# Two-block transformer kernel on one core: a gate tile computed beside memory attention, weight chunks sent before modulation rows, and the opening pairs of tiles taken one by one

## The chip, the cores and the metric

One NeuronCore of a Trainium2 chip. The time is the device time of one launch in microseconds. The kernel before takes 3383.51 us (median of 3 runs, 3382.79 to 3384.63).

## The reference, cut to what matters

A first block of two layers and a second block of two layers, all in fp32, for 512 positions of width 1024.

```
# first block, each of 2 layers
h = x @ w_in[l]                          # split into the inputs of four branches, their gates, and merge
y_mem = memory attention(xq, mem)        # 4 heads, 512 queries against 256 memory tokens
proj  = einsum('bsnc,ncd->bsnd', branches, w_o_branch[l])
gates = sigmoid(merge.reshape(B, S, 4, D) + b_gate[l])
merged = sum(gates * proj, axis=2);  out = merged @ w_out[l]
x = layer_norm(alpha * x + out)
# second block, each of 2 layers: x (512 rows) and a context (256 rows)
mod = silu(c) @ w_ada[i] + b_ada[i]      # for x and, with c_ctx, for the context
hx = rms_norm(x) * (1 + sc1) + sh1;  zx = hx @ w_in[i]     # q, k, v, pool and fourier inputs
hc = the same of the context;        zc = hc @ w_in[i]     # layer 1: its k and v only
x = x + ga1 * (mix(zx) @ w_out[i])
x = x + ga2 * swiglu(rms_norm(x) * (1 + sc2) + sh2)        # layer 0: the context too
```

## The kernel before, in words

**Three matmuls for one.** Activations lie transposed, 128 channels to a tile, 512 positions (256 for the context) along the free axis. Each fp32 operand is split into a rounded `high` and the rest, `low`, and a product is high x high + high x low + low x high, summed in a PSUM bank. A tile of 128 output channels over 1024 inputs is 8 k-steps of 3, 24 matmuls. `with_high` (L153) issues the two that need the weights' high alone, `three` (L161) all three in a row.

**The stream of weights** (L93). All weights lie in memory as one sequence of chunks of 128x1024, in the order of use. SP loads them into a ring of 3 (`send`, L105), and waits with chunk n for the low of chunk n-3. ACT makes a chunk's high (`hi`, L115, L123), POOL its low (`lo`, L126, L131). Highs and lows have two buffers each, so the high of a chunk waits until the next-but-one before it is done with: TensorE counts `used` up with the first matmul of each chunk, and the split of the s-th chunk waits until the chunk after the (s-2)-th has started. Each engine works through its own instructions in the order in which they are written, and every stage is a block that starts when all engines are done with the last one.

**Memory attention** (`attention`, L275, called at L1590): 8 pairs of heads and query blocks. TensorE makes the scores two pairs ahead (L330), DVE the maximum (L447), ACT the exponent (L384), DVE the inverse of the sum (L453), POOL multiplies by it (L428), TensorE turns the probabilities round (L343), ACT and DVE copy them out (L393, L463), TensorE forms the product (L357) and DVE evicts and gates it (L468). Scores use PSUM banks 0 to 3, turns 4 and 5, products 6 and 7 in turn. POOL first gates the convolution branch (L1583). Another attention of the kernel passes `beside`, tiles of 24 matmuls put between its steps in three pieces, and then uses bank 6 alone for products.

**Merge** (L1618): for each of 8 output tiles m, four gates (24 matmuls each, `gemm3`, L670, over x) and two chunks of branch projections, n = 0, 1 and n = 2, 3 (L1653 to L1661), in the order gate, gate, projections, gate, gate, projections; chunks lie in that order (`chunks1`, L2816). ACT first splits the branches (L1672), which DVE completes (L1707), then applies the sigmoids (L1683) with the splits of later chunks between (L1684); at i = 0 it also splits branches 8 to 15 and applies `Silu` to the two condition vectors (L1692). DVE multiplies and adds (L1718, L1723), and between these works through 48 modulation rows (512 KB each, L1731). SP sends the rows (L1634) into four buffers, a row when DVE has used up the one four before, and a weight chunk ahead of most rows (L1629).

**Second block, input stage** (L2200 on). ACT makes the norm's scale, then for each of 8 tiles DVE normalises (L2125), ACT shifts and rounds to the high (L2105), DVE makes the low (L2133); all of x's tiles come before the context's. In layer 0 only x is done so, the context was done earlier. `first_pair` (L2138) runs the first two output tiles of x as these arrive; then come tiles 2 to 10 (L2272), each waiting for its chunk's low, with the context's products beside x's (layer 1: from tile 4 on). ACT evicts each tile (L2354) and makes a chunk's high after that (L2376). `used` for the pair's second chunk is counted with its last matmul.

**Feed-forward** (L2680 on): the same norm (`norm.scalar`, L2107) and `first_pair`, for x and the context in layer 0 and for x in layer 1, then pairs of gate and up tiles (L2711); ACT applies `Silu` (L2729).

## Time and profile before

| | |
|---|---|
| median of 3 runs | 3383.51 us |
| profiled execution | 3376.45 us |
| its span, first to last instruction | 3374.7 us |
| mean granted TensorE clock | 0.989 |
| TensorE busy | 3210.8 us (95%) |
| VectorE (DVE) | 1502.5 us (45%) |
| ScalarE (ACT) | 1185.3 us (35%) |
| GpSimd (POOL) | 1494.4 us (44%) |

Times are microseconds from the start of the span. PE is TensorE, L12 is line 12 of the kernel. A timeline row has the start, the length, the engine, the line and the operation, output <- inputs, how many instructions were merged, and in brackets how long the engine had been idle before it and what ended that. Matmuls overlap: each is shown with its whole length, so eight 128x512 matmuls that start 0.23 us apart are shown with 0.39 us each. A granted clock of 1.00 is TensorE's 2.4 GHz, 0.50 is 1.2 GHz.

### The profile page before, as it was taken

How to read it: one execution, taken by the hardware profiler on the slowest of the kernel's cores; microseconds unless marked ns; L12 is line 12 of the kernel's file. 1: busy time of each engine (PE TensorE's matmuls, PEld its weight loads, DVE VectorE, ACT ScalarE, POOL GpSimd, SP SyncE). 2: the span in 40 equal slices, each digit the busy share in tenths (PEclk: the TensorE clock that was granted, in tenths of full speed). 3: DMA queues.
4: the chain of work that ended last, by engine and by line, in shares of the span. 5: the costliest groups of instructions: out<-in, count | busy, mean ns of one | idle time of the engine just before them, and what ended most of it. 6: DMA issues, size and time to landing. Idle time of an engine off the chain costs nothing. (4 is left out here: it accounts for less than half of the span.)

```text
span 3374.7 us, 51787 instructions
## 1 busy us (share of the span) xinstructions
PE 3210.8 (95%) x21120; PEld 2520.3 (75%) x21120; DVE 1502.5 (45%) x2374; ACT 1185.3 (35%) x1940; POOL 1494.4 (44%) x820
## 2 busy tenths in 40 slices
PE   8899999999999999989998989999999988899999
PEld 6784786788668747868886756888888865678787
DVE  7643374899575332948986235300100022620000
ACT  6224434422352434252225445322122233532221
POOL 4432553455353235535543276344234424745454
PEclk9999999999999999999999999999999999999999
DMA  3011132555210111335543200121122211023232
GB/s 129 8 34 56 57 100 68 207 200 194 80 63 4 46 56 57 106 109 191 206 150 109 72 26 26 51 68 60 54 74 65 63 54 50 7 88 96 92 99 94
DMA packets 77611, 284.18 MB, mean 84 GB/s; under 512 B 8736, under 2 KB 8736, under 8 KB 76864
## 3 DMA queue, kind: packets, MB, share of 16 engines
q1 hardware_dynamic: 77376, 280.88, 24.9%
q8 instruction: 168, 2.75, 0.3%
q14 instruction: 67, 0.55, 0.1%
HBM read 278.75 MB, written 2.10 MB: 83 GB/s over the span
## 5 line engine op out<-in xcount | busy, mean ns | idle before, releaser
L131 POOL TENSOR_TENSOR lows<-ring,highs 128x1024 fp32r<-128x1024 f32 x376 | 946.3, 2518 | 1555.5 <-ACT highs L123 1519.5
L155 PE MATMUL ps<-x_high,highs 128*128 128x512 f32 x1936 | 772.4, 399 | 32.7 <-ACT highs L123 14.1
L158 PE MATMUL ps<-x_low,highs 128*128 128x512 f32 x1936 | 759.9, 393 | 0.0
L123 ACT ACTIVATE highs<-ring 128x1024 fp32r<-128x1024 f32 x376 | 396.9, 1056 | 742.4 <-PE ps L155 382.1
L155 PEld LDWEIGHTS ps<-x_high,highs 128*128 128x128 f32 x1936 | 366.4, 189 | 124.3 <-issue 29.3
L158 PEld LDWEIGHTS ps<-x_low,highs 128*128 128x128 f32 x1936 | 366.4, 189 | 78.2 <-issue 2.9
L1731 DVE CUSTOM_DVE_ANT_0 BR<-BR 128x1024 f32<-128x1024 f32 x144 | 282.6, 1963 | 6.8
L2762 DVE TENSOR_TENSOR hidden_scratch<-ps,hidden_scratch 128x512 f32<-128x512 f32 x44 | 30.4, 691 | 545.9 <-PE ps L2081 541.9
L677 PE MATMUL ps<-x_high,lows 128*128 128x512 f32 x1040 | 256.9, 389 | 0.0
L677 PEld LDWEIGHTS ps<-x_high,lows 128*128 128x128 f32 x1040 | 195.2, 188 | 40.6
L2638 DVE SCALAR_TENSOR_TENSOR BR<-ps,mod,BR 128x512 f32<-128x512 f32 x72 | 47.4, 661 | 368.8 <-PE ps L167 368.8
L167 PE MATMUL ps<-hidden_parts,lows 128*128 128x512 f32 (+1 forms) x528 | 188.9, 358 | 0.0
L163 PE MATMUL ps<-hidden_parts,highs 128*128 128x512 f32 (+1 forms) x528 | 188.8, 358 | 0.0
L166 PE MATMUL ps<-hidden_parts,highs 128*128 128x512 f32 (+1 forms) x528 | 188.8, 358 | 0.0
L428 POOL TENSOR_SCALAR tiles<-tiles 128x768 f32<-128x768 f32 (+1 forms) x80 | 155.0, 1950 | 27.9 <-DVE tiles L453 27.9
L2081 PE MATMUL ps<-x_high,lows 128*128 128x512 f32 x672 | 167.1, 391 | 0.0
L1558 DVE SCALAR_TENSOR_TENSOR ps<-X,par,ps 128x512 f32<-128x512 f32 x232 | 152.9, 751 | 0.0
L2081 PEld LDWEIGHTS ps<-x_high,lows 128*128 128x128 f32 x672 | 123.3, 188 | 24.0
L428 POOL TENSOR_SCALAR X<-X 128x256 f32<-128x256 f32 (+3 forms) x96 | 97.8, 1033 | 66.2 <-DVE X L453 66.2
L447 DVE TENSOR_REDUCE tiles<-ps 128x1 f32<-128x768 f32 (+1 forms) x80 | 67.6, 846 | 108.7 <-PE ps L330 108.5
L1683 ACT ACTIVATE BR<-ps,par 128x512 f32<-128x512 f32 x64 | 44.1, 689 | 201.2 <-PE ps L677 201.1
L166 PEld LDWEIGHTS ps<-hidden_parts,highs 128*128 128x128 f32 x528 | 99.4, 188 | 16.1
(437 smaller groups left out, 5847.0 us busy)
## 6 DMA issues: line engine op xcount, KB each, us to landing
ring<-in_w SPq DMA_DIRECT2D x414, 512.0 KB, 3.5
BR<-in_ada SPq DMA_DIRECT2D x72, 512.0 KB, 3.5
merging<-in_ada SPq DMA_DIRECT2D x24, 512.0 KB, 3.5
X<-in_xT SPq DMA_DIRECT2D x4, 512.0 KB, 6.8
X<-in_memT SPq DMA_DIRECT2D x2, 1024.0 KB, 5.5
BR<-in_cond SPq DMA_DIRECT2D x4, 512.0 KB, 5.4
out<-BR SPq DMA_DIRECT2D x8, 256.0 KB, 4.4
cst<-in_cst SPq DMA_DIRECT2D x1, 1408.0 KB, 7.9
```

The lines of the kernel that those rows point to most:

```text
L123: nc.scalar.activation(self.high(n), self.chunk(n), ACT.Copy).then_inc(self.hi_made, 1)
L131: nc.gpsimd.tensor_tensor(self.low(n), self.chunk(n), self.high(n).bitcast(F32), ALU.subtract).then_inc(self.lo_made, 1)
L155: mm = nc.tensor.matmul(ps, high, xhigh, start=start, stop=False)
L158: nc.tensor.matmul(ps, high, xlow, start=False, stop=False)
L163: mm = nc.tensor.matmul(ps, high, xhigh, start=start, stop=False)
L166: nc.tensor.matmul(ps, high, xlow, start=False, stop=False)
L167: return nc.tensor.matmul(ps, low, xhigh, start=False, stop=stop)
L428: nc.gpsimd.tensor_scalar(prob(i, u), prob(i, u), stats[:, 3, n:n + 1], None, ALU.mult).then_inc(S("normed"), 1)
L677: mm = nc.tensor.matmul(PS[:, bank, :], tile_of(stream.low(n), k), xh[:, k, :], start=False, stop=(k == DK - 1))
L1558: ins = v.scalar_tensor_tensor(out=ACC[:, c, :] if tap == TAPS - 1 else acc, in0=H0[:, c, tap:tap + T], scalar=w, in1=acc, op0=ALU.mult, o ...
L1731: v.tensor_tensor_reduce(PROD, rows_of(t), CB[:, c, :], 1.0, 0.0, ALU.mult, ALU.add, AD[:, t, c:c + 1]).then_inc(S("ada"), 1)
L2081: mm = nc.tensor.matmul(ps, tile_of(stream.low(n), k), high[:, k, :], start=False, stop=(k == DK - 1))
```

## The change

1. `attention` takes `ahead`. For memory attention that is the first gate tile of the merge (m = 0, branch 0), in three pieces of 8 matmuls into PSUM bank 7: two ahead of the scores of pair 2 and of pair 3, the third (its lows) ahead of the turns of pair 7. SP sends two more chunks in that stage, ACT makes one high (i = 0) and POOL one low (between pairs 6 and 7). Products then use bank 6 alone.
2. In the merge the first gate is left out and its sigmoid reads bank 7. The chunks of m = 0 lie in the order gate, gate, gate, projections, gate, projections. SP sends each weight chunk one step earlier relative to the modulation rows. `Silu` on the condition comes after the sigmoid of i = 2.
3. `first_pair`: for the last stream the two tiles run one after the other, from k = 4 on for x alone and from k = 0 for the context, and `used` is counted when the second one starts alone.
4. `norm.scalar` makes the third chunk's high right after the shifted tiles of a stream (`between`), and in layer 1's input stage evicts x's first two tiles there, before the context's shifted tiles.
5. Tiles 2 to 10 of the input stage run their 16 (with the context 32) matmuls with the weights' high first and wait for the low after them.

```diff
+class Ahead:
+        self.at = {(0, 0): 0, (0, 1): 1, (8, 1): 2}
+    def send(self, sp):
+        self.stream.send(sp, self.first + RING + 1)
+    def tensor(self, pe, i, slot):
...
+        if part < 2:
+            stream.wait_high(pe, n)
+            for k in range(4 * part, 4 * part + 4):
+                with_high(self.nc, bank, tile_of(stream.high(n), k), self.high[:, k, :], self.low[:, k, :], k == 0, stream.used if k == 0 else None)
+        else:
+            stream.wait_split(pe, n)
+            for k in range(DK):
+                self.nc.tensor.matmul(bank, tile_of(stream.low(n), k), self.high[:, k, :], start=False, stop=(k == DK - 1))
+    def scalar(self, act, i):
+        if i == 0:
+            self.stream.hi(self.nc, act, self.first + 2)
+    def pool(self, pool, i):
+        if i == 6:
+            self.stream.lo(self.nc, pool, self.first + 2)
...
-        return 6 if beside is not None else 6 + g % 2
+        return 6 if beside is not None or ahead is not None else 6 + g % 2
...
-                if beside is not None and p.group >= 1:
+                if (beside is not None or ahead is not None) and p.group >= 1:
                     pe.wait_ge(S("out"), p.group)
...
         def gate_chunk(i):
-            return n0 + 6 * (i // 4) + 3 * (i % 4 // 2) + i % 2
+            return n0 + (0, 1, 2, 4)[i] if i < 4 else n0 + 6 * (i // 4) + 3 * (i % 4 // 2) + i % 2
+        def branch_chunk(m, n):
+            return n0 + 6 * m + 3 * (n // 2) + 2 if m else n0 + 3 + n
+        def splits_ahead(i):
+            return (n0 + 4, n0 + 5, n0 + 6, n0 + 8)[i] if i < 4 else min(gate_chunk(i) + (4 if i % 2 else 3), n0 + 48 + 1)
...
-                    stream.send(sp, n0 + RING + max(45 * t // 48, min(t, 2)))
+                    stream.send(sp, n0 + RING + max(45 * t // 48 + 1, min(t + 2, 4)))
...
-                        for i in (4 * m + n, 4 * m + n + 1):
+                        for i in ((4 * m + n, 4 * m + n + 1) if m else (1, 2) if n == 0 else (3,)):
...
-                stream.hi(nc, act, gate_chunk(1) + 1)
+                stream.hi(nc, act, n0 + 3)
...
-                    act.wait_ge(S("gate_product"), i + 1)
+                    if i:
+                        act.wait_ge(S("gate_product"), i)
...
-                    stream.hi(nc, act, min(gate_chunk(i) + (4 if i % 2 else 3), n0 + 48 + 1))
+                    stream.hi(nc, act, splits_ahead(i))
...
                     if i == 0:
                         for b in range(8, 16):
                             branch_high(b)
+                    if i == 2:
                         act.wait_ge(S("cond"), 32)
                         nc.scalar.activation(CB, CB, ACT.Silu).then_inc(S("silu_c"), 1)
...
-                for s in self.sts:
+                for i, s in enumerate(self.sts):
                     self.shifted(act, s)
+                    if i == between:
+                        stream.hi(nc, act, upto + 1)
+                        for take in then:
+                            take()
...
                 for i, s in enumerate(sts):
-                    for k in range(DK):
+                    final = i == len(sts) - 1
+                    half = DK if not final else 4 if i == 0 else 0
+                    for k, j in [(k, j) for k in range(half) for j in range(2)] + [(k, j) for j in range(2) for k in range(half, DK)]:
...
-                            if j == 1 and i == len(sts) - 1 and k == DK - 1:
+                        if j == 1 and final and k == half:
                                 mark = used
...
-                    stream.wait_split(pe, n)
-                    first = True
+                    stream.wait_high(pe, n)
+                    taking = []
...
-                            mm = three(nc, PS[:, s["bank"] + i % 2, 0:s["n"]], tile_of(stream.high(n), k), tile_of(stream.low(n), k),
-                                       s["h"][:, k, :], s["l"][:, k, :], k == 0, k == DK - 1, mark(n, first))
+                            with_high(nc, bank, tile_of(stream.high(n), k), s["h"][:, k, :], s["l"][:, k, :], k == 0, mark(n, k == 0 and not taking))
+                        taking.append((s, bank))
+                    stream.wait_split(pe, n)
+                    for s, bank in taking:
+                        for k in range(DK):
+                            mm = nc.tensor.matmul(bank, tile_of(stream.low(n), k), s["h"][:, k, :], start=False, stop=(k == DK - 1))
+                        mm.then_inc(S("product" + s["name"]), 1)
...
-                norm.scalar(act, n0 + PARTS)
+                norm.scalar(act, n0 + PARTS, 0, () if layer == 0 else (lambda: evict(streams[0], tiles[0]), lambda: evict(streams[0], tiles[1])))
...
-                        norm.scalar(act, n0 + PARTS)
+                        norm.scalar(act, n0 + PARTS, len(full) - 1)
```

## Rows read from the trace of the kernel before

**Rows 1.** The page: its first line and TensorE's part of section 1.
```profile
span 3374.7 us, 51787 instructions
...
PE 3210.8 (95%) x21120; PEld 2520.3 (75%) x21120; DVE 1502.5 (45%) x2374; ACT 1185.3 (35%) x1940; POOL 1494.4 (44%) x820
```
**Rows 2.** TensorE's waits: us in total, times, longest.
```profile
PE ps L155 <- ACT highs L123: 17.5, 9, 7.4
```
**Rows 3.** Timeline of TensorE, memory attention of layer 0.
```profile
560.66 1.97 PE L330 MATMUL ps<-X 128*128 128x256 f32 x8 [1.26 <-PEq L1459]
563.59 2.17 PE L330 MATMUL ps<-X 128*128 128x256 f32 x8 [0.96 <-ACT X L384]
...
567.45 0.44 PE L343 MATMUL ps<-cst,X 128*128 128x128 f32 x2 [0.46 <-POOL X L428]
...
581.09 0.44 PE L343 MATMUL ps<-cst,X 128*128 128x128 f32 x2 [1.33 <-POOL X L428]
...
585.25 1.13 PE L357 MATMUL ps<-X 128*128 128x128 f32 x8 [0.63 <-issue]
```
**Rows 4.** Timeline of TensorE, start of the merge of layer 0.
```profile
587.42 0.61 PE L155 MATMUL ps<-x_high,highs 128*128 128x512 f32 x1 [1.05 <-PEq L314]
...
592.76 1.98 PE L677 MATMUL ps<-x_high,lows 128*128 128x512 f32 x8
594.58 0.39 PE L155 MATMUL ps<-x_high,highs 128*128 128x512 f32 x1
...
607.34 0.50 PE L155 MATMUL ps<-x_high,highs 128*128 128x512 f32 x1 [1.54 <-ACT highs L123]
```
**Rows 5.** Timeline, input stage of the second block's layer 0, DVE and TensorE.
```profile
1858.20 1.62 DVE L2133 SCALAR_TENSOR_TENSOR x_low<-tiles,mod,x_high 128x512 fp32r<-128x512 f32 x2
...
1865.64 0.50 PE L163 MATMUL ps<-x_high,highs 128*128 128x512 f32 x1 [3.37 <-POOL lows L131]
```
**Rows 6.** Timeline, input stage of the second block's layer 1, ACT and TensorE.
```profile
2746.57 0.91 ACT L2105 ACTIVATE context_high<-tiles,mod 128x256 fp32r<-128x256 f32 x2 [1.22 <-DVE tiles L2125]
...
2752.40 0.58 ACT L2354 ACTIVATE tiles<-ps 128x512 f32<-128x512 f32 x1
...
2756.39 0.79 PE L163 MATMUL ps<-x_high,highs 128*128 128x512 f32 x1 [6.18 <-POOL lows L131]
...
2769.96 0.39 PE L163 MATMUL ps<-x_high,highs 128*128 128x512 f32 x1
```
**Rows 7.** Timeline, feed-forward openings of layers 0 and 1, TensorE and DVE.
```profile
2163.65 3.83 PE L2142 MATMUL ps<-highs 128*128 128x512 f32 x10 [1.88 <-PEq L2650]
...
2184.18 0.49 DVE L2133 SCALAR_TENSOR_TENSOR context_low<-BR,mod,context_high 128x256 fp32r<-128x256 f32 x1 [0.19 <-ACT context_high L2105]
...
2187.33 0.50 PE L155 MATMUL ps<-x_high,highs 128*128 128x512 f32 x1 [1.31 <-ACT highs L123]
...
3017.58 0.50 PE L155 MATMUL ps<-x_high,highs 128*128 128x512 f32 x1 [0.95 <-ACT highs L123]
```
**Rows 8.** Timeline of ACT, merge of layer 0.
```profile
606.24 1.05 ACT L123 ACTIVATE highs<-ring 128x1024 fp32r<-128x1024 f32 x1
```
**Rows 9.** Timeline of POOL, end of attention and start of the merge, layer 0.
```profile
580.11 3.63 POOL L428 TENSOR_SCALAR X<-X 128x256 f32<-128x256 f32 x4 [1.65 <-DVE X L453]
588.60 2.39 POOL L131 TENSOR_TENSOR lows<-ring,highs 128x1024 fp32r<-128x1024 f32 x1 [4.86 <-ACT highs L123]
```
**Rows 10.** Busy time by stretch: us, each engine busy (instructions), clock, DMA, GB/s.
```profile
587.40:590.80 3.40, 3.38 (x8) 2.64 (x9) 1.73 (x1) 3.34 (x6) 2.21 (x1) 0.53 0.49 148
...
1532.00:1770.00 238.00, 237.90 (x1036) 194.16 (x1035) 217.37 (x241) 66.37 (x79) 117.23 (x42) 1.00 0.51 181
```
**Rows 11.** Timeline of SP and TensorE, tenth tile of the merge of layer 0.
```profile
629.61 0.43 SPq L112 DMA_DIRECT2D ring<-in_w  x1
...
644.17 1.98 PE L677 MATMUL ps<-x_high,lows 128*128 128x512 f32 x8
```
**Rows 12.** DMA issues from 587 to 625 us: count, KB each, median us to landing.
```profile
ring<-in_w SPq DMA_DIRECT2D x7, 512.0 KB, 4.5
```

More of the change, by code:

```diff
@@ L272, in pool, with __init__, attention @@
         self.stream.lo(self.nc, pool, self.first + min(piece // 3, len(self.places) - 1) + 2)
-def attention(nc, stage, PS, ident, causal, pairs, results, scale, probs, probsT, small, gates=None, opening=None, beside=None):
+class Ahead:
+    def __init__(self, nc, stream, bank, first, high, low):
+        self.nc, self.stream, self.bank, self.first, self.high, self.low = nc, stream, bank, first, high, low
+        self.at = {(0, 0): 0, (0, 1): 1, (8, 1): 2}
+    def send(self, sp):
+        self.stream.send(sp, self.first + RING + 1)
+    def tensor(self, pe, i, slot):
+        if (i, slot) not in self.at:
+            return
+        stream, n, bank, part = self.stream, self.first, self.bank, self.at[i, slot]
+        if part < 2:
[12 more added lines that the diff above has]
+            self.stream.lo(self.nc, pool, self.first + 2)
+def attention(nc, stage, PS, ident, causal, pairs, results, scale, probs, probsT, small, gates=None, opening=None, beside=None, ahead=None):
     S, other = stage()
@@ L318, in _ @@
                 beside.send(sp)
+            if ahead is not None:
+                ahead.send(sp)
             clear(sp, other)
@@ L362, in _ @@
             for i in range(N + 2):
+                if ahead is not None:
+                    ahead.tensor(pe, i, 0)
                 if i + lead < N:
@@ L366, in _ @@
                     beside.tensor(pe, S, 2 * i)
+                if ahead is not None:
+                    ahead.tensor(pe, i, 1)
                 if 1 <= i <= N:
@@ L370, in _ @@
                     beside.tensor(pe, S, 2 * i + 1)
+                if ahead is not None:
+                    ahead.tensor(pe, i, 2)
                 if i >= 2:
@@ L405, in _ @@
                     exponent(i + 1)
+                if ahead is not None:
+                    ahead.scalar(act, i)
                 if beside is not None:
@@ L430, in _ @@
                     beside.pool(pool, 2 * i + 1)
+                if ahead is not None:
+                    ahead.pool(pool, i)
         @block.vector
@@ L1592, in first @@
                   128.0 ** -0.5, [XT(0), XT(1), XT(2)], [XT(4), XT(5)], XT(14),
-                  [GLATER[:, 4 + 2 * (g // 2):6 + 2 * (g // 2), 256 * (g % 2):256 * (g % 2) + 256] for g in range(4)], gate_conv)
+                  [GLATER[:, 4 + 2 * (g // 2):6 + 2 * (g // 2), 256 * (g % 2):256 * (g % 2) + 256] for g in range(4)], gate_conv,
+                  ahead=Ahead(nc, stream, PS[:, 7, :], base + FIRST["merge"], XH, XL))
         room.close()
@@ L2145, in first_pair @@
                 for i, s in enumerate(sts):
[L2146 removed]
+                    final = i == len(sts) - 1
+                    half = DK if not final else 4 if i == 0 else 0
+                    for k, j in [(k, j) for k in range(half) for j in range(2)] + [(k, j) for j in range(2) for k in range(half, DK)]:
                         self.ready(pe, s, k)
[L2148 to L2155 removed]
+                        mark = opened if j == 0 and i == 0 and k == 0 else None
+                        if j == 1 and final and k == half:
+                            mark = used
+                        mm = three(nc, PS[:, s["bank"] + banks[j], 0:s["n"]], tile_of(stream.high(n + j), k), tile_of(stream.low(n + j), k),
+                                   s["h"][:, k, :], s["l"][:, k, :], k == 0, k == DK - 1, mark)
+                        if k == DK - 1:
+                            mm.then_inc(done(j, s), 1)
             def ready(self, pe, s, k):
@@ L2373, in _ @@
                     for s in streams:
-                        if t in plan[s["name"]] and not (layer == 0 and s["name"] == "c" and j < EARLY):
+                        if t in plan[s["name"]] and not (layer == 0 and s["name"] == "c" and j < EARLY) and not (layer and j < 2):
                             evict(s, t)
```

21 lines of the change are left out of this document (8 added, 13 removed).

## The prediction

> **What bounds the kernel now.** I read the page first: TensorE is busy for 3210.8 of 3374.7 us [rows 1]. So only what fills a TensorE gap, or keeps its clock up, can pay; the matmuls themselves stay the same in number. Second, TensorE's waits, by who ended them: ACT's `highs` cost the streamed gemms 17.5 us in 9 waits [rows 2]: late splits of weight chunks. Third, the timeline at the places that the diff touches. In memory attention TensorE waits in small pieces: 0.96, 0.46, 1.33 and 0.63 us among them [rows 3], about 5.4 us in all over 26 us. In the merge stage it waits 1.54 us once [rows 4]. In the second block's input stage it waits 3.37 us in layer 0 [rows 5] and 6.18 us in layer 1 [rows 6]; at the two opening pairs of the feed-forward 1.31 and 0.95 us [rows 7]. The last number to take along is the pitch of a 128x512 matmul at full clock: eight from 592.76 to 594.58 make 0.2275 us each [rows 4]; a tile of 24 is 5.46 us.
>
> **Part 1, the gate tile beside attention, in both layers of the first block.**
> Removed from the merge: 24 matmuls, 5.46 us. Removed too: the wait of 1.54 us. There a high was made at 606.24 only, behind `Silu` and two table loads [rows 4, 8]. The change moves `Silu` behind two more sigmoids and two more highs, and sends chunk n0+3 in the stage before. By my estimate (from the stage's start, with the durations of ACT's rows), ACT then makes the highs of n0+3, n0+4, n0+5 at 9.5, 15.5 and 17.2 us, where TensorE wants them at 10.9, 16.5 and 21.9; `Silu` ends at 20.4, and n0+6 is ready at 25 for 27.5. So the wait should not come back; the least room is 1 us, at n0+4, where the weights queue behind the two condition vectors.
> Added to attention: the same 24 matmuls in three pieces of 8 (1.82 us each), one split on ACT (1.05) and one on POOL. The first two pieces stand ahead of the scores of pairs 2 and 3. TensorE was free at 562.6; two pieces and two pairs of scores (2.0 us) end at 568.2, the first two transposes at 568.6, where the next stood at 567.45 [rows 3]. Delay: 1.15 us, and from there TensorE had no rest for 7 us, so it is passed on. The third piece and POOL's split come at the end. POOL is the one that is waited for there: its normalisations of pairs 6 and 7 run back to back in 3.63 us, and the transpose at 581.09 waits for them [rows 3, 9]. The split is put between the two and takes 2.39 us [rows 9], so pair 7, its transposes and its product come 2.3 us later; the third piece fits into that wait at no cost of its own. Stage longer by 1.15 + 2.3 = 3.4 us; bounds 0 (all in the gaps) and 5.46 (nothing hidden). I take 3.4. The single output bank (6 alone, since 7 holds the gate) makes the products of a new group wait for the eviction before; those waits of about half a microsecond fall where TensorE waits for POOL anyway.
> Sum: 5.46 + 1.54 - 3.4 = 3.6 us a layer, **7.2 us** for two.
> After the gap at the stage's start the granted clock was 0.53 for 3.4 us, the 1.2 GHz level; TensorE had stood still for 0.63 and 1.05 us before and done little between [rows 3, 4, 10]. Eight matmuls at 0.427 instead of 0.2275 cost 1.6 us. I leave that in place, as the gap stays; if it goes, 3.2 us more for two layers.
>
> **Part 2, the opening pairs.** `first_pair` used to alternate its two tiles over k; now the last stream's second tile (all of it for the context, k 4 to 7 for a lone x) runs when the first is done. Its mark allows the split of the third chunk, and comes some 11 matmuls before the end instead of at the end. `norm.scalar` makes that split before anything else, and the input stage no longer waits for `lows` before a tile's first 16 matmuls. The price: TensorE must wait for the last k of the first tile, then still has 12 matmuls (24 for the context) to do.
> Layer 0, input: the last x_low ends at 1859.82 [rows 5]. After 0.05 us (a high that ended at 607.29 let TensorE start at 607.34 [rows 4, 8]) come 3 and 12 matmuls, 3.4 us: the pair ends at 1863.3, 1.2 us later than before, and the third tile starts there, its high made since 1862.1. Before it started at 1865.64. Gain **2.4 us**.
> Layer 1, input: TensorE lagged here, so the pair ends as before, at 2750.2 less what the pipeline overlaps (2756.39 - 6.18) [rows 6]. The third tile follows at once and ends at 2755.5. But ACT now evicts x's second tile (done 2750.25, 0.5 us) **before** the context's eight shifted tiles, which took from 2746.57 to 2752.40, 5.83 us [rows 6]. They end at 2756.6, then comes the fourth chunk's high, 1.05: the fourth tile starts at 2757.65, after a new wait of 2.1 us, and the fifth at 2763.1, where it was 2769.96 [rows 6]. Gain **6.8 us**. Part of it is clock: that third tile took 8.1 us for 24 matmuls before (2769.96 - 5.46 - 2756.39), 2.7 more than at full clock.
> Feed-forward, layer 0: the context's last low ends at 2184.67; 3 + 24 matmuls of half width (half of 0.2275) make 3.1, so the third tile starts at 2187.8 against 2187.33 [rows 7]: **loss 0.5 us**, though its wait of 1.31 is gone. Layer 1: the pair is 1.2 us longer as in layer 0's input, the wait of 0.95 goes: **0**, between -0.3 and +0.2.
> Moving lows behind highs also makes both streams' products of a tile end close together; evictions come later by up to 1.9 us. TensorE needs them a tile later, with two banks a stream: nothing.
> The clock again. A gap of 1.88 us was followed by ten matmuls in 3.83 us, 0.38 each, mostly the lower level [rows 7]; after the one of 3.37 us the next began no slower [rows 5]. So the new wait of 2.1 us may or may not cost a stretch of 1.7 us; I take half of it, 0.9.
> The Trainium skill (TensorE: Matmul & The Clock Gate, HAM oscillation) blames long unbroken gaps alone for the lower level; by that rule the new wait costs nothing and the sum would be 0.9 larger. The rows disagree with a rule by length alone: the longer gap cost less than the shorter.
>
> **Sum:** 7.2 + 2.4 + 6.8 - 0.5 - 0 - 0.9 = **15.0 us**. The profiled execution took 3376.45 us (span 3374.7), 7.1 below the median of the timed runs, 3383.51; the terms are differences within it, so I take them off both: 3361.5 for a profiled one, **3368.5 us** for the median.
>
> **Rivals.**
> (A) The gate tile is not hidden: attention grows by the whole 5.46, as TensorE's pieces hold up scores on which DVE, ACT and POOL all wait. For it: the gaps are all shorter than a piece of 1.82 us. Against: POOL's chain at the end leaves 1.33 and the split's 2.3. Gain 15.0 - 4.1 = 10.9: 3372.6. With the clock also lost at the feed-forward's context pair (1.7, as TensorE rests there half of 4 us) and the whole stretch at the new wait: 3375.
> (B) The clock holds at both merges and at the new wait: 15.0 + 3.2 + 0.9: 3364.4.
> (C) TensorE outruns its weights in the merge. They are sent between modulation rows, which go out as DVE uses them up. In the tenth tile of the stage the chunk sent at 629.61 landed 4.5 us later, was wanted at 640.5 (644.17 less 16 matmuls) and needs 1.05 for its high: room 5.4 us [rows 11, 12]. TensorE gains 7.0 on this, `Silu` starts 3.5 later, one send ahead gives back a row's time, about 5: room -0.1 if DVE makes up nothing; but it idled for 20.6 of 238 us [rows 10], so 2 or 3 us are left. If it bites, it gives back up to 3 a layer: 3374.5.
> (D) Slower: the rows starve. SP now waits for a later chunk's low before each row, and all 44 paced rows of a layer queue behind that wait. Each wait that is not covered delays DVE's modulation sums. DVE has 20.6 us to spare in the merge [rows 10], and 7.5 a layer must be lost to undo the gains; so it decides from (20.6 + 7.5)/44 = 0.64 us a row. At 1 us a row the kernel loses 23.4 - 7.5 a layer, 32 in all: 3415. Against it: 4 row buffers, and by my count the low in question is made two tiles before DVE wants the row.
> (E) The change does not do what it says: the splits were hidden anyway and only the order differs. Excluded in the input stages by their waits; for the feed-forward pairs I already count it so.
>
> **Numbers.** Forecast 0.58, A 0.16, B 0.12, C 0.09, D 0.05. About 0.2% (6.8 us) is what a measurement of this kernel can tell from no change. A and C together can fall into it: same 0.08; D gives slower 0.05; faster 0.87. The range takes in B with a shorter attention (2 x 1.5 more) at 3361 and A with C at 3377; the bounds 0 and 5.46 of the attention term lie inside.
>
> **What would show it.** Attention 3.4 us longer in each layer, its two split matmul pieces ahead of scores. No wait of 1.54 in the merge, none for a high in its first six tiles. In layer 0's input stage the third tile right behind the pair; in layer 1 no wait of 6.18 but one of some 2.1 before the fourth tile, ended by ACT's highs. In the feed-forward's opening, TensorE waiting in pieces for context_low and the third tile no earlier. I am wrong if attention is as long as before or 5 us longer, if DVE waits for rows, or if SP's queue makes ACT wait for the ring.

## The result, and the profile after

| | kernel before | changed kernel |
|---|---|---|
| first measurement, median | 3384.07 us (3382.79 to 3388.82, 4 runs) | 3361.91 us (3359.74 to 3364.15, 4 runs) |
| second measurement, median | 3384.05 us (3376.86 to 3394.47, 24 runs) | 3365.16 us (3362.82 to 3368.75, 6 runs) |
| profiled execution, span | 3376.45, 3374.7 us | 3363.31, 3361.5 us |

The ratio is 0.9932, 95% interval 0.9915 to 0.9949, in the first measurement and 0.9943, 0.9928 to 0.9957, in the second: 22 and 19 us less. The profiled pair differs by 13.2 us of span only. How the three figures go together is told under "What the runs showed of the hardware".

First the page of the changed kernel, as in [rows 1], and TensorE's wait for ACT's `highs`, as in [rows 2]:

```profile
span 3361.5 us, 51793 instructions
...
PE 3210.8 (96%) x21120; PEld 2519.1 (75%) x21120; DVE 1510.7 (45%) x2374; ACT 1184.6 (35%) x1940; POOL 1490.9 (44%) x820
```
```profile
PE ps L155 <- ACT highs L123: 17.5, 9, 7.4
```

TensorE's busy time is the same 3210.8 us to the tenth: no work was saved, gaps were. And the wait that the change was aimed at stands at 17.5 us in 9 waits as before. A sum of waits is a poor witness here. Four of the nine are gone (1.54 twice, 1.31, 0.95 us) and four new ones have come (1.13, 1.09, 0.54, 2.01 us, shown below); the waits for POOL's `lows`, 9.5 us before, are what left the list.

So I read it by stage instead. The length of a stage here is the time from TensorE's first instruction in it to its first in the next, from the timelines:

| stage | before | after | measured | forecast |
|---|---|---|---|---|
| memory attention, layer 0 / 1 | 26.76 / 26.76 | 29.56 / 29.57 | +2.80 / +2.81 | +3.4 each |
| merge, layer 0 / 1 | 276.32 / 276.32 | 267.47 / 270.93 | -8.85 / -5.39 | -7.0 each |
| input stage, layer 0 | 131.05 | 128.87 | -2.18 | -2.4 |
| input stage, layer 1 | 98.35 | 93.12 | -5.23 | -6.8 + 0.9 |
| feed-forward to its last up tile, layer 0 / 1 | 285.42 / 189.23 | 286.00 / 189.28 | +0.58 / +0.05 | +0.5 / 0 |
| sum | | | **-15.4** | -15.0 |

The other stages, which the change doesn't touch, became 2.2 us longer in this pair; they have 63 us at the lower clock where the kernel before has 48.

The timeline of TensorE in the changed kernel's memory attention, layer 0, against [rows 3]:

```profile
560.56 1.97 PE L365 MATMUL ps<-X 128*128 128x256 f32 x8 [1.27 <-PEq L1504]
562.18 0.58 PE L155 MATMUL ps<-x_high,highs 128*128 128x512 f32 x1
...
568.23 1.03 PE L365 MATMUL ps<-X 128*128 128x256 f32 x4
...
579.56 1.13 PE L392 MATMUL ps<-X 128*128 128x128 f32 x8 [0.78 <-DVE BR L513]
...
581.60 0.44 PE L378 MATMUL ps<-cst,X 128*128 128x128 f32 x2 [0.69 <-POOL X L471]
...
582.90 2.09 PE L297 MATMUL ps<-x_high,lows 128*128 128x512 f32 x8
585.76 0.44 PE L378 MATMUL ps<-cst,X 128*128 128x128 f32 x2 [0.78 <-POOL X L471]
...
587.94 1.13 PE L392 MATMUL ps<-X 128*128 128x128 f32 x8 [0.63 <-issue]
590.12 0.47 PE L155 MATMUL ps<-x_high,highs 128*128 128x512 f32 x1 [1.05 <-PEq L347]
```

The gate tile's pieces start at 562.18 without a gap; L378 are the turns, L392 the products, L297 the third piece, with a wait for POOL's normalisation before it (0.69 us, at 581.60) and after it (0.78 us). At 579.56 the single output bank shows: a wait of 0.78 us for DVE's eviction. The last row is the start of the merge. POOL in the same stretch, against [rows 9]:

```profile
580.62 1.83 POOL L471 TENSOR_SCALAR X<-X 128x256 f32<-128x256 f32 x2 [1.43 <-DVE X L498]
582.41 2.40 POOL L131 TENSOR_TENSOR lows<-ring,highs 128x1024 fp32r<-128x1024 f32 x1
584.79 1.82 POOL L471 TENSOR_SCALAR X<-X 128x256 f32<-128x256 f32 x2
```

The low parts the normalisations of pairs 6 and 7, and the turns at 585.76 follow the second of them. Now TensorE at the openings of the two input stages, against [rows 5, 6]:

```profile
1854.29 0.50 PE L163 MATMUL ps<-x_high,highs 128*128 128x512 f32 x1 [0.36 <-DVE x_low L2193]
...
1858.70 0.39 PE L155 MATMUL ps<-x_high,highs 128*128 128x512 f32 x1
...
2747.31 1.98 PE L2366 MATMUL ps<-x_high,lows 128*128 128x512 f32 x8
2751.29 0.74 PE L155 MATMUL ps<-x_high,highs 128*128 128x512 f32 x1 [2.01 <-ACT highs L123]
2751.82 0.63 PE L158 MATMUL ps<-x_low,highs 128*128 128x512 f32 x1
```

In layer 0 the third tile (1858.70) follows the pair with no wait; the 3.37 us are gone. In layer 1 the 6.18 us are gone, and a new wait of 2.01 us stands before the fourth tile, with matmuls of 0.63 us behind it: the lower clock.

### The profile page after: what moved, and what is told of

Read it like the earlier page. It is cut to its first block and busy times, and to the rows that moved or that the text cites. A ratio compares the mean times of both kernels' runs of the same rounds, so it can differ in the third digit from the quotient of the medians.

```text
span 3361.5 us, 51793 instructions
## 1 busy us (share of the span) xinstructions
PE 3210.8 (96%) x21120; PEld 2519.1 (75%) x21120; DVE 1510.7 (45%) x2374; ACT 1184.6 (35%) x1940; POOL 1490.9 (44%) x820
## 3 DMA queue, kind: packets, MB, share of 16 engines
q1 hardware_dynamic: 77376, 280.88, 24.4%
## 5 line engine op out<-in xcount | busy, mean ns | idle before, releaser
L155 PE MATMUL ps<-x_high,highs 128*128 128x512 f32 x2080 | 832.4, 400 | 32.1 <-ACT highs L123 13.5
L158 PE MATMUL ps<-x_low,highs 128*128 128x512 f32 x2080 | 815.9, 392 | 0.0
L155 PEld LDWEIGHTS ps<-x_high,highs 128*128 128x128 f32 x2080 | 393.3, 189 | 130.7 <-issue 35.2
L158 PEld LDWEIGHTS ps<-x_low,highs 128*128 128x128 f32 x2080 | 393.4, 189 | 85.5 <-issue 4.8
L1787 DVE CUSTOM_DVE_ANT_0 BR<-BR 128x1024 f32<-128x1024 f32 x144 | 290.4, 2017 | 6.8
L166 PEld LDWEIGHTS ps<-hidden_parts,highs 128*128 128x128 f32 x528 | 99.4, 188 | 16.1
L163 PEld LDWEIGHTS ps<-hidden_parts,highs 128*128 128x128 f32 x528 | 99.4, 188 | 16.1
```

What stands on the lines that cost most here:

```text
L155: mm = nc.tensor.matmul(ps, high, xhigh, start=start, stop=False)
L158: nc.tensor.matmul(ps, high, xlow, start=False, stop=False)
L163: mm = nc.tensor.matmul(ps, high, xhigh, start=start, stop=False)
L166: nc.tensor.matmul(ps, high, xlow, start=False, stop=False)
L1787: v.tensor_tensor_reduce(PROD, rows_of(t), CB[:, c, :], 1.0, 0.0, ALU.mult, ALU.add, AD[:, t, c:c + 1]).then_inc(S("ada"), 1)
```

## The experiments

All kernels are compared with the kernel before on the same chip. Experiments 5 to 10 are one execution each. Against the kernel before on their chip they took, in this order, 17.1, 22.1, 19.3, 17.2, 18.5 and 16.2 us less (3381.20 us once for 5, 6, 7 and 9, a median of 3384.75 for 8 and 10); the changed kernel itself ran from 3359.7 to 3368.8 us, so these totals don't tell the edits apart. Each is read by the length of the stages that its edit touches, against the first profile of the changed kernel.

**1 and 2. Each half alone.** `gate_only` has the gate tile, the order of chunks, the sends and the place of `Silu`; `opening_only` has the rest (`first_pair`, `norm.scalar`, the tiles of the input stage).

```diff
# gate_only keeps, of the changed kernel:
+                  ahead=Ahead(nc, stream, PS[:, 7, :], base + FIRST["merge"], XH, XL))
# opening_only keeps:
+                    half = DK if not final else 4 if i == 0 else 0
```

> The kernel before with the gate tile beside memory attention and the changed sends and order of the merge, and with the opening pairs and the input stages as they were. My theory: attention 2.8 us longer and the merge 8.8 (layer 0) and 5.5 us (layer 1) shorter, as in the profile of the changed kernel, so 8.5 to 9 us less than before; 5 to 6 of it if the clock falls at the merges' starts again. Rival (the gate tile's 24 matmuls are not hidden and the gain is in the opening pairs): 3 us less.

> The kernel before with the changed opening pairs, splits and evictions of the second block alone. My theory: input stages 2.2 us (layer 0) and 5.2 us (layer 1) shorter, the feed-forward opening of layer 0 0.5 us longer, that of layer 1 even: 6 to 8 us less than before. Rival (the new order of the pairs costs as much as the earlier split brings): 0 to 3 us less.

Measured: `gate_only` 3373.21 us, ratio 0.9972 (0.9954 to 0.9990), 10.8 us less; attention 29.56, merge 267.44 and 270.93 us, the same as in the changed kernel. The rival of 3 us is out by these lengths. The median gained somewhat more than the 8.5 to 9 us expected, but its interval runs from 3 to 16 us. TensorE's waits in it still have the input stages':

```profile
PE ps L163 <- POOL lows L131: 9.5, 2, 6.2
```

`opening_only` 3375.82 us, ratio 0.9969 (0.9958 to 0.9980), 8.2 us less; input stages 128.88 and 93.55, feed-forward 286.01 and 189.28. The rival (0 to 3 us) is outside the interval, 6.8 to 14.2 us. The two parts add up: 10.8 + 8.2 = 19.0, beside the 18.9 of the whole. So close an agreement is luck with intervals as wide as these; what shows that the parts share no cover is that the stages that each half touches have, within 0.5 us, the length that they have in the changed kernel.

**3 and 4. Both kernels again**, unchanged.

> The kernel before, unchanged, profiled a second time. The first profiled execution took 3376.45 us, the timed ones 3382.8 to 3388.8. Theory 1 (that one profiled execution happened to have fewer stretches at the lower clock level than most): the ratio to the kernel before is 1.000 within 0.002, and single executions scatter over some 8 us, with the granted clock of the stretches after gaps differing from one to the next. Theory 2 (the timed executions differ from the profiled ones in something else): the profile is again near 3376 while the times stay near 3384.

> The changed kernel, unchanged. Its first profiled execution took 3363.3 us, 13.1 less than the profiled one of before, while the medians lie 22 us apart. Theory 1 (the change is worth the 13 to 15 us that the terms give, and the rest is how the chip happened to grant the clock to the executions compared): 12 to 17 us less than before here. Theory 2 (the change gains 22 us, for instance by clock stretches that only some executions of before have): 20 us or more less.

Measured: the kernel before 3385.29 us, ratio to itself 1.0004 (0.9992 to 1.0015); the changed one as in the table above, 18.9 us less. The first pair of theories is decided: the ratio is 1.000, and the profiled execution took 3391.88 us, not 3376 again; single executions scatter over 15 to 18 us, though, not over 8. The second pair isn't: 18.9 us lies between the 12 to 17 of one and the 20 of the other, and its interval, 14.6 to 24.4 us, holds both. The value is in the second profile of the kernel before, span 3390.1 us where the first had 3374.7. TensorE in its merge of layer 0, against the wait of 1.54 us in [rows 4]:

```profile
609.31 0.50 PE L155 MATMUL ps<-x_high,highs 128*128 128x512 f32 x1 [3.17 <-ACT highs L123]
609.64 0.52 PE L158 MATMUL ps<-x_low,highs 128*128 128x512 f32 x1
609.96 0.63 PE L155 MATMUL ps<-x_high,highs 128*128 128x512 f32 x1
```

This merge began at full clock (it was granted up to 609.8), and the wait is 1.6 us longer for it: the high comes when ACT comes to it, however early TensorE is. So in the kernel before a lower clock at the merge's start costs nothing, since the wait swallows it; and after the longer wait the lower clock came anyway (0.63 us a matmul), which makes this merge 277.92 us where the first profile has 276.32.

**5. The pair's second tile alone later** (`pair_split_later`).

```diff
-                    half = DK if not final else 4 if i == 0 else 0
+                    half = DK if not final else 6 if i == 0 else 4
```

> The changed kernel with the opening pairs split later: x alone from k = 6 instead of 4, the context from k = 4 instead of 0. My theory (the changed pair ends late because the second tile's matmuls come after the last low, and the third tile only needs its high about 2.2 us after that low): the layer 0 feed-forward stage 1.2 us shorter than in the changed kernel (286.0 from its first matmul to that of the second half), the layer 0 input stage 1.0 us shorter (128.9), the layer 1 feed-forward 1.0 us (189.3), the layer 1 input stage the same within 0.3 apart from the clock. Rival (the early mark is what counts, and a later split brings the wait for highs back): each 0 to 1 us longer.

Measured: 3364.12 us. Feed-forward 285.60 and 188.79: 0.4 and 0.5 us less. Input stage of layer 0 130.45, of which a stretch of lower clock ahead of the pair is 1.8; of layer 1 91.48, with no lower clock behind its wait. A new wait appears there, before the third tile:

```profile
2745.45 0.47 PE L155 MATMUL ps<-x_high,highs 128*128 128x512 f32 x1 [0.65 <-ACT tiles L2419]
```

The third tile goes to the bank of the first, and now comes before ACT has evicted that (L2419). Layer 0's input stage has the same wait (0.91 us), and gains 0.2 us instead of 1.0: in the input stages the end of the pair is worth less than I thought, since the eviction is next in line. In the feed-forward the gain here is a third to a half of the expected 1.2 and 1.0, but experiment 11 has the same edit of the pair and there these stages are 1.2 and 0.9 us shorter. No wait for the eviction stands in either. The stretches at the lower clock lie differently in the two executions (in layer 0 from 5.6 us into the stage here, from 0.9 us there; in layer 1 6.8 us long here, 3.4 there); that this is the reason was not tested.

**6. The fourth chunk's high amid the context's tiles** (`context_after_high`), in `norm.scalar` for the second stream.

```diff
                 for i, s in enumerate(self.sts):
+                    if i and then:
+                        self.shifted(act, s, 0, 4)
+                        stream.hi(nc, act, upto + 2)
+                        self.shifted(act, s, 4)
+                        continue
                     self.shifted(act, s)
```

> The changed kernel with the fourth chunk's high made between the fourth and the fifth of the context's shifted tiles, in layer 1's input stage. My theory (the wait of 2.01 us before the fourth tile is ACT's order: two evictions and eight shifted tiles stand before that high): that wait goes, and the stretch at the lower clock after it, so the stage (93.1 us from its first matmul to the next stage's) is 2.0 us shorter, 3.6 if the clock stays. Rival (the weights' arrival or DVE sets that high): no difference, and if the context's last tiles come late, a wait at the fifth tile.

Measured: 3359.07 us; the stage 89.44 us, 3.7 less than in the changed kernel. ACT, then TensorE:

```profile
2746.02 0.51 ACT L2161 ACTIVATE context_high<-tiles,mod 128x256 fp32r<-128x256 f32 x1 [0.28 <-DVE tiles L2190]
2746.43 1.05 ACT L123 ACTIVATE highs<-ring 128x1024 fp32r<-128x1024 f32 x1
2747.38 0.89 ACT L2161 ACTIVATE context_high<-tiles,mod 128x256 fp32r<-128x256 f32 x2
```
```profile
2746.71 1.98 PE L2371 MATMUL ps<-x_high,lows 128*128 128x512 f32 x8
2748.52 0.39 PE L155 MATMUL ps<-x_high,highs 128*128 128x512 f32 x1
```

Against the third tile's last eight matmuls the high starts 0.3 us before (2746.43 to 2746.71) instead of 2.9 us behind (2750.20 to 2747.31). The fourth tile follows the third without a wait, and the 2.0 us of wait and the 1.7 us of lower clock behind it are both gone. ACT's tiles of 0.51 us came 0.79 apart, waiting for DVE each time, so the high fitted into time that ACT didn't use.

**7. POOL's low one pair earlier** (`low_before_pair6`).

```diff
-        if i == 6:
+        if i == 5:
             self.stream.lo(self.nc, pool, self.first + 2)
```

> The changed kernel with POOL's split of the second gate chunk put before the normalisations of pair 6 instead of those of pair 7. My theory (memory attention is 2.8 us longer because that split of 2.4 us stands between two normalisations that are waited for, while POOL idles 1.65 us before pair 6): attention 28.3 us instead of 29.56 in each layer, 2.5 us in all. Rival (the first two matmul pieces before the scores make the stage longer): no difference.

Measured: 3361.92 us; attention 29.44 and 29.45, 0.12 us less a layer. The forecast failed. POOL did as it should; TensorE shows why it doesn't pay:

```profile
580.32 2.35 POOL L131 TENSOR_TENSOR lows<-ring,highs 128x1024 fp32r<-128x1024 f32 x1
582.65 3.63 POOL L471 TENSOR_SCALAR X<-X 128x256 f32<-128x256 f32 x4
```
```profile
583.63 0.44 PE L378 MATMUL ps<-cst,X 128*128 128x128 f32 x2 [1.55 <-POOL X L471]
...
584.94 2.09 PE L297 MATMUL ps<-x_high,lows 128*128 128x512 f32 x8
586.87 0.38 PE L378 MATMUL ps<-cst,X 128*128 128x128 f32 x2
```

The wait for the low moved with it, from pair 7's turns to pair 6's (1.55 us), while the third piece stayed ahead of pair 7's turns, where nothing is waited for any more: it stands unhidden. Here low and piece cover each other only in the same gap.

**8. Both moved** (`low_and_piece`): the edit above, and

```diff
-        self.at = {(0, 0): 0, (0, 1): 1, (8, 1): 2}
+        self.at = {(0, 0): 0, (0, 1): 1, (7, 1): 2}
```

> The changed kernel, but in memory attention POOL makes the gate chunk's low between pairs 5 and 6 instead of 6 and 7, and TensorE takes the tile's third piece ahead of pair 6's turns instead of pair 7's. My theory after low_before_pair6: there POOL ended 1.5 us earlier, but the third piece then stood unhidden ahead of pair 7's turns, and pair 6's turns waited 1.55 us for POOL; the low and the piece have to move together. Expected: attention 28.0 us in each layer (29.56 in the changed kernel, 26.76 before), all else as in the changed kernel. Rival: the low costs POOL's chain its 2.4 us wherever it stands ahead of the last pair, and the piece covers nothing new: attention stays at 29.4 to 29.6.

Measured: 3367.55 us; attention 28.94 and 28.93, 0.6 us less a layer, between the theory's 28.0 and the rival's 29.4. TensorE at the end:

```profile
585.07 0.44 PE L378 MATMUL ps<-cst,X 128*128 128x128 f32 x2 [0.22 <-POOL X L471]
586.12 1.13 PE L392 MATMUL ps<-X 128*128 128x128 f32 x8 [0.62 <-ACT X L434]
...
588.11 1.13 PE L392 MATMUL ps<-X 128*128 128x128 f32 x8 [0.63 <-issue]
```

The wait for POOL has shrunk to 0.22 us, and next in line are ACT's copies of the turned blocks (L434), 0.62 us. So moving low and piece is worth 0.6 us here. Attention is still 2.2 us longer than in the kernel before; how that divides between the pieces, the low and the copies was not separated.

**9. The next high ahead of the wait for the merged tile** (`high_before_merged`). In the changed kernel's merge of layer 1 TensorE waits three times for a high, which it didn't before. One of these places, ACT, then TensorE:

```profile
1570.80 0.63 ACT L1742 ACTIVATE merged_high<-BR 128x512 fp32r<-128x512 f32 x1 [8.21 <-DVE BR L1779]
1571.34 0.67 ACT L1738 ACTIVATE BR<-ps,par 128x512 f32<-128x512 f32 x1
1571.91 1.04 ACT L123 ACTIVATE highs<-ring 128x1024 fp32r<-128x1024 f32 x1
```
```profile
1573.10 0.47 PE L155 MATMUL ps<-x_high,highs 128*128 128x512 f32 x1 [1.13 <-ACT highs L123]
```

ACT stood still for 8.21 us, waiting for DVE to finish the merged tile, with the sigmoid and the high queued behind that wait. The other two places look the same: ACT waits 7.22 and 7.62 us for the merged tile, then TensorE 1.09 and 0.54 us for the high. In the kernel before ACT waits there too, 34.7 us in 12 with 4.9 at most, and TensorE doesn't.

```diff
                     if i >= 4 and i % 4 == 0:
+                        stream.hi(nc, act, splits_ahead(i) + 1)
                         act.wait_ge(S("merged"), 3 * i // 4)
```

> The changed kernel, where at each output tile of the merge ACT makes one chunk's high more before it waits for DVE's merged tile. My theory (the waits of 1.13, 1.09 and 0.54 us in layer 1's merge come from ACT standing in the wait for the merged tile, up to 8.2 us, as DVE is behind with its modulation sums): these waits go, that stage 2.8 us shorter than 270.9, layer 0's merge unchanged at 267.4 (269.1 with the lower clock at its start). Rival (the ring is late, since SP sends weights between rows as DVE uses them up): the same waits remain, put down to the ring.

Measured: 3362.70 us; merge of layer 1 267.44 us, 3.5 us shorter where I expected 2.8, with none of the three waits. ACT's wait for DVE's merged tile, in the changed kernel and then in this one:

```profile
ACT merged_high L1742 <- DVE BR L1779: 81.6, 14, 8.2
```
```profile
ACT merged_high L1743 <- DVE BR L1780: 9.7, 9, 2.6
```

The gain doesn't show in the single time, since layer 0's merge (269.10) had the lower clock at its start and layer 1's input stage 10.2 us of it in its opening (94.22). The three waits stood in layer 1 in all seven profiles that have the gate tile and the changed sends without this edit, and in layer 0 in one of them (`low_and_piece`: 271.08); with it, in none of four merges (two in this kernel, two in `all_four`).

**10. Sends at the old pace** (`sends_as_before`).

```diff
-                    stream.send(sp, n0 + RING + max(45 * t // 48 + 1, min(t + 2, 4)))
+                    stream.send(sp, n0 + RING + max(45 * t // 48, min(t + 2, 4)))
```

> The changed kernel, but from the fifth modulation row on SP sends the weight chunks at the pace of the kernel before (45 t / 48), one later than the changed kernel does; the first rows keep the changed order. This asks what the third part of the title, weights sent ahead of the rows, buys. My theory, after high_before_merged: the stalls of layer 1's merge come from DVE's lag through ACT's order, not from late loads, so the send order buys nothing outside the first tiles: merge stages 267.4 and 270.9 us, as in the changed kernel, with its three short waits in layer 1, each within 0.5 us. Rival (the prediction's C): the room was used up by the shorter stage, so without the earlier send TensorE waits for ACT's highs and ACT for the ring's loads, in the middle tiles: merge stages 2 us or more longer in each layer, and ACT's waits for DMA grow from near nothing to over 3 us a layer.

Measured: 3368.59 us; merges 271.13 and 270.03. My theory was wrong here and the rival right in kind for a late weight chunk: ACT now waits for one, and TensorE for ACT. But in layer 1 the stage is 0.9 us shorter than in the changed kernel, which neither foresaw.

```profile
627.86 1.06 ACT L123 ACTIVATE highs<-ring 128x1024 fp32r<-128x1024 f32 x1 [9.56 <-DMA ring<-in_w]
```
```profile
629.06 0.47 PE L155 MATMUL ps<-x_high,highs 128*128 128x512 f32 x1 [1.77 <-ACT highs L123]
```

It happens once a layer, 35 to 37 us into the stage (1.77 and 1.79 us), not all along it. Inside the two merges ACT's waits for the ring are 43.1 us in 10, where the changed kernel has 12.4 in 4 and the kernel before 4.3 in 1. The three waits of experiment 9 are absent here, but for one of 0.30 us in layer 1. So the earlier sends take away a wait of 1.8 us a layer, but in layer 1 the three waits that stand in their kernel cost more (2.76 us): they pay in layer 0 and, as long as experiment 9's edit is missing, not in layer 1. Of layer 0's 3.7 us, 1.6 are the lower clock at the stage's start. Sends at the old pace together with experiment 9's edit were not run.

**11. All four together** (`all_four`): experiments 5, 6, 8 and 9 in one kernel.

> The changed kernel with all that the single runs bore out: the low between pairs 5 and 6 with the third piece ahead of pair 6's turns; in the merge the next high ahead of the wait for DVE's merged tile; in layer 1's input stage the fourth chunk's high amid the context's shifted tiles; and the opening pairs' second tile starting alone later (k 6 for a lone x, k 4 for the context). Expected from the single runs, each against the changed kernel's 3363.3 us profiled: attention -1.5 in each of two layers, merge of layer 1 -3.5, layer 1's input stage -3.7, opening pairs -1.1 in three stages together (-0.2, -0.4, -0.5): 11.3 us less, so a ratio to the kernel before of 0.9943 - 0.0033 = 0.991, some 3354 us beside 3384. The rival is that the parts share one cover: they sit in different stages, so they should add up, except in layer 1's input stage, where the pair and the high meet: there the gain could be 2 us smaller, 0.9916.

Measured: 3353.72 us (3352.49 to 3356.78, 4 runs) against 3384.75, ratio 0.9911 (0.9894 to 0.9927): 31 us less than before, and some 8 to 11 us less than the changed kernel by its two medians, which were taken on other occasions. Attention 28.97 and 28.96, merge 267.47 and 267.46, input stages 130.74 and 90.46, feed-forward 284.79 and 188.37. The time is the 3354 us that I expected, but the terms are not: attention gave 0.6 us a layer where I had 1.5, the input stage of layer 1 2.7 instead of 3.7 (the third tile's wait of 0.65 us from experiment 5 and a further stretch of lower clock in the opening), the feed-forward 2.1 instead of 0.9; the input stage of layer 0 is 1.9 longer, with 3.4 us at the lower clock and a wait of 0.91 us for the eviction; only the merge of layer 1 gave its 3.5. The touched stages are 7.6 us shorter in all, not 11.3, so that the total agrees is partly luck. TensorE's waits for ACT's highs, 17.5 us in 9 in the kernel before and in the changed one, now:

```profile
PE ps L155 <- ACT highs L123: 12.4, 5, 7.5
```

## Why the prediction was right, and where it was off

The forecast was 3368.5 us and the range 3361 to 3377; the medians are 3361.9 and 3365.2. The direction and the places and mechanisms of the gains hold; new waits in layer 1's merge were missed. Both medians lie nearer to rival B's 3364.4 than to the forecast. B's condition, full clock at both merges, was met in the first profile and not in the second, and at the new wait in neither. Stage by stage the sum is 15.4 us against 15.0; but layer 0's merge gained 1.9 us more and layer 1's 1.6 us less than forecast, and attention cost 1.2 less in both layers together where the second input stage gained 0.7 less; so the sum agrees better than its terms, and that part is luck.

- **Attention, two pieces ahead of scores.** I took 1.15 us of delay. The scores behind the turns of [rows 3], at 567.72 before (the first row below), start at 568.23: 0.5 us. The first piece begins at 562.18, while the last scores are still running (I had it begin when they end, 562.6), and four turns run back to back in 0.44 us, where I let the first two take 0.4. Error 0.6 us a layer.
- **Attention, the low between pairs 6 and 7.** 2.3 us forecast; 2.80 - 0.5 leaves 2.3. The rows say the same: from pair 6's turns to pair 7's it was 1.80 us before (581.09 of [rows 3] to the second row below) and is 4.16 now (581.60 to 585.76), 2.36 more. That the third piece costs nothing of its own holds for this place, not for the one tried in experiment 7.

```profile
567.72 1.03 PE L330 MATMUL ps<-X 128*128 128x256 f32 x4
...
582.89 0.44 PE L343 MATMUL ps<-cst,X 128*128 128x128 f32 x2 [0.25 <-POOL X L428]
```

- **Merge.** 5.46 + 1.54 = 7.0 us was right for equal clocks: `after_again`, whose merge starts at the lower clock as the kernel before's did, has 269.07, 7.25 less. In the first profile the stretch was absent and the merge 8.85 shorter; rival B had 7.0 + 1.6 = 8.6. The step that failed is "I leave that in place": whether it comes is a matter of the execution. And rival B had the right reason for counting it: only with the wait gone does the clock there change the time.
- **Merge of layer 1, new waits.** 2.76 us, forecast as "none". I had followed ACT's order for the first tiles only. The step missing was what stands ahead of the high from i = 4 on, at every fourth i: the wait for DVE's merged tile. DVE is busy for 253.60 us of the 265 from 1495 to 1760, so it has little to catch up with. Experiment 9 shows the step. Why layer 1 has these waits and layer 0 mostly hasn't stays open (see the last section).
- **Rival C**, weights that come late, did not reach TensorE. One of my signs of being wrong did show: ACT waits for the ring inside the merges, 12.4 us in four waits, the longest 5.7, where it waited 4.3 us once before; but no wait of TensorE follows these. With the old pace of sends one does (experiment 10), at 1.8 us a layer where I priced up to 3. **Rival D**, rows that starve, did not happen: in the trace DVE never waits for a row in the merges. **Rival A** is out: attention grew by 2.8, not 5.46. For A with C together I wrote 3377 as the range's end; my own prices, 4.1 and 6 us off the gain, give 3378.6.
- **Input stage of layer 0.** 2.4 forecast, 2.18 measured. Where the old 3.37 us were followed by the lower clock the gain is larger: 4.8 against the second profile of the kernel before (133.67 us), 3.8 against `gate_only` (132.63).
- **Input stage of layer 1.** 5.9 net forecast; 5.23 here, 5.51 and 5.27 between the other pairs of profiles (98.82 to 93.31; 98.82 to 93.55). The new wait is 2.01 us where I had 2.1, and the clock stretch behind it came in whole, 1.7, where I took half. That accounts for the difference.
- **Feed-forward.** +0.5 and 0 forecast, +0.58 and +0.05 measured.
- **From the profiled pair to the median.** I took the differences of one profiled execution off the median. The interval of the second measurement holds 15.4 us (it runs from 14.6 to 24.4 us), that of the first doesn't (17.3 to 28.8). The second pair of profiles, `before_again` and `after_again`, differs by 28.5 us: 19.6 in the stages of the table and 8.9 in stages that nothing changed. So a good part of what one comparison shows beyond the sum has nothing to do with the change; that the clock accounts for all of it is not shown.

## What to carry to other kernels

When a wait in a saturated stream is removed, look at what the same engine's queue has further on: here the high's maker (ACT) had a wait for a slower engine ahead of it, which cost TensorE nothing in the kernel before, and moving one split ahead of that wait gave the 3.5 us back. Work put beside other work is best put in the very gap that its own input opens: here low and third piece moved together gained, the low alone hardly. And judge differences under half a per cent by the length of stages and by medians of many runs, never by one pair of profiles or by the sum of a wait.

## What the runs showed of the hardware that I had not expected

**The clock differs between executions of one program.** The kernel before ran from 3376.9 to 3394.5 us in 24 runs. Its two profiles, spans 3374.7 and 3390.1, have TensorE at its lower level, 1.2 GHz, for 72 and 106 us in all; the two of the changed kernel have 76 and 69. The same gap goes either way: at the merge's start TensorE stood still for 1.05 us in every profile, and the matmuls after it were at full clock in the one of `gate_only` and fell to the lower one in `after_again`; the 3.37 us of [rows 5] were followed by full clock in the first profile of the kernel before and by the lower one in the second and in `gate_only`. The Trainium skill (TensorE: Matmul & The Clock Gate, HAM oscillation) blames long unbroken gaps; the gap of 2.0 to 2.3 us before the fourth tile was followed by the lower clock in seven of the eight profiles that have it and by full clock in `pair_split_later`, and that of 3.37 us once was not followed by the lower one, so length alone doesn't settle it here.

**A removed wait can pay twice where a stretch at the lower clock follows it**: 3.7 us in experiment 6, for a wait of 2.0. That is one execution; in `all_four` the same wait is gone, but a stretch at the lower clock stands at another place of that stage.

**One pair of profiles misjudges such a difference.** The mean granted clock is 0.986 and 0.988 in the two middle runs of the kernel before's 24, and 0.989 to 0.991 in the six of the changed one. The first profile of the kernel before, at 0.989, was among its best executions, and in it the stages that nothing changed were 7.8 us shorter than in the second. That goes the right way for 13 us by the first pair of profiles and 19 to 22 by the medians; an exact account it is not.

**DVE and POOL make each other wait, and the one that starts first is not slowed.** DVE's modulation sum over 128x1024 and POOL's low of the same size in the merge of layer 1, changed kernel:

```profile
1562.23 1.22 DVE L1787 CUSTOM_DVE_ANT_0 BR<-BR 128x1024 f32<-128x1024 f32 x1
...
1563.49 3.29 DVE L1787 CUSTOM_DVE_ANT_0 BR<-BR 128x1024 f32<-128x1024 f32 x1
...
1566.93 1.23 DVE L1787 CUSTOM_DVE_ANT_0 BR<-BR 128x1024 f32<-128x1024 f32 x1
```
```profile
1562.68 3.03 POOL L131 TENSOR_TENSOR lows<-ring,highs 128x1024 fp32r<-128x1024 f32 x1 [2.79 <-ACT highs L123]
```

The first sum runs beside the low from 1562.68 to 1563.45 and still takes 1.22 us. The middle one starts when the low is already running, and takes 3.29: it ends 1.1 us after the low, which ends at 1565.71. The low in turn began while the first sum ran, and takes 3.03 us instead of the 2.40 that it took in attention. This holds for all 192 sums of the two merges of the changed kernel. The 80 that began while an instruction of POOL was running took 2.08 to 3.40 us and ended 1.08 to 1.09 us behind it; the 65 during which one of POOL began, and the 47 beside none, all took 1.21 to 1.23. So DVE's load in the merge depends on how lows and sums fall together: its sums (L1787, with the short reads of their results) are busy for 191.06 us in layer 0's merge and 194.80 in layer 1's, with the same instructions. The Trainium skill (GPSIMD Engine Reference, Specifications) says that GpSimd shares its SBUF interfaces with VectorE, with contention where VectorE has two inputs there; the sum reads a row and the condition from SBUF, and the rows agree and give the size.

The three waits of experiment 9 go with this load. In the eight merges that have them (layer 1 in seven profiles, layer 0 in `low_and_piece`) the sums without these reads add up to 194.0 to 194.2 us; in every other merge of the thirteen profiles to at most 190.7. That is a likely reason why they stand in one layer and mostly not in the other. Which of the two brings the other about, and what sets the load, was not tested.
